# GpSimd splits the weights block by block: order of the halves, constant waits, no gate operation

## The chip, the core and the metric

The kernel runs on one core of one Trainium2 chip. A core has five engines that run at the same time and meet only through semaphores: TensorE (PE in the profile, with PEld for its weight loads) multiplies matrices, VectorE (DVE), ScalarE (ACT) and GpSimd (POOL) work on rows of elements, and SyncE (SP) issues transfers from the chip's main memory. The metric is the device time of one execution in microseconds (us).

## The reference

A decoder of two layers on 512 positions of width 1024, in float32. Each layer has a feed-forward of width 2816, a mixer, a cross-attention into 256 memory positions, and another feed-forward:

```python
for layer in range(DEPTH):
    h = h + 0.5 * swiglu(rmsnorm(h, ffn1_norm[layer]), ...)
    hn = rmsnorm(h, mix_norm[layer])
    if layer % 2 == 0:
        mix = concatenate([gla_mixer(...), s5_mixer(...)]) @ ev_w_out
    else:
        mix = dsa_mixer(hn, ...)            # indexer, top-k, attention
    h = h + mix
    h = h + cross_attn(rmsnorm(h, xa_norm[layer]), mem_n, ...)
    h = h + 0.5 * swiglu(rmsnorm(h, ffn2_norm[layer]), ...)
return rmsnorm(h, final_norm)
```

## The kernel before

**Weights.** All weights come as one stream of 381 blocks of 128 x 1024 float32 (512 KB), in the order of use. A block goes into one of two slots of `raw`, block b into slot b % 2, in two halves of 512 columns, called a and b here. For exactness each weight is split in two: a high part in the fp32r format and a low part, the rest. `W` has two slots as well, each with a high and a low part. A product then is three matmuls (`mm3`, L338 to L340: high by high, high by low, low by high), so an ordinary block is 8 x 3 = 24 matmuls of 512 columns.

**Who does what.** SyncE loads a half of `raw` as soon as GpSimd has split the same half of the block two earlier. GpSimd splits: a TENSOR_SCALAR (L308) writes the high part, a TENSOR_TENSOR (L312) the low part, with a wait on the first between them. Before both stands the gate, a TENSOR_TENSOR on one column (L307), behind the two waits: for the load, and for TensorE to be done with this half of the block two earlier. Four semaphores count halves in order: `half_split` and `split_ready` (a and b halves split), `half_done` and `block_done` (a and b halves used up by TensorE).

**The order of GpSimd.** Two blocks at a time: a of the even, a of the odd, b of the even, b of the odd. Block 108 (`LONE`) stands alone, and the pairs behind it begin with an odd block. Both parts are loops at run time, 53 and 136 turns, whose waits are against registers. SyncE's reloads have the same loops and order.

**The order of TensorE.** Most blocks are used one after the other, a then b (`tile`, `down`, `kv_tile`); TensorE waits for `half_split` at the start and for `split_ready` in the middle. In three places it is otherwise. `project` begins each projection with two blocks interleaved, for k = 0 to 7 both in turn, as the normalised input comes ready in pieces k (`x_lo`), and it waits for the a halves of both first:

```python
pe.wait_ge(S("half_split"), at + 2)
...
for k in range(KC):
    if k == KC // 2:
        pe.wait_ge(split_ready, at + 2)
    pe.wait_ge(S("x_lo"), X_LO_NORM[n] + k + 1)
    for t in range(min(2, nt)):
        m = tile_k(BANKS[t], (at + t) % 2, x, k, k == 0, k == KC - 1)
```

The last two of the 22 down blocks of a feed-forward are interleaved in the same way over the eight output banks, so that the outputs come ready one by one and VectorE can begin the next normalisation (`norm`: L1384 adds to h, L1359 writes the low part of x, L1369 adds squares). The feed-forwards begin at blocks 0, 125, 191 and 315 and have 66 blocks each; behind the first stands the projection of the even mixer (66), behind the second the third feed-forward (191), behind the third the projection of the odd mixer (257). And `glu` (blocks 88 and 89) takes one half block for each of its four outputs.

**The memory keys and values.** `kv_tile` works on 256 columns (the memory), so its matmuls are half as long. Of the first layer, blocks 83 to 87 (keys) come behind the mixer's projections, then `glu`, then three more (90 to 92), then singly between the parts of the gated linear attention (`gla`). ScalarE copies each out of its bank (L1072), and behind the fifth key it computes the decays (L1098), on which VectorE waits (L1682); then come the sigmoids of `glu`.

**The start.** `load(0, a)`, part of x, the vectors, `load(1, a)`, `load(0, b)`, `load(1, b)`, and then the rest of x and the constants.

Of the kernel before, what the change touches and what calls it, by code (L numbers as in the profile page):

```python
# [31 lines left out]
ALU = mybir.AluOpType  # L32
# [3 lines left out]
P = 128  # L36
# [8 lines left out]
HALF = BLK // 2  # L45
# [40 lines left out]
LONE = XQ_AT[0] - 1  # L86
OD_AT, OD_TILES = 257, 16
OD_V_AT = 273
N_BLOCKS = 381
# [88 lines left out]
def build_trunk(nc, xT, memT, pos, vecs, w_alpha, s5b, s5bt, s5c, blocks, mats, mask, rows, stream, out):  # L178
    with ExitStack() as ctx:
        def sb(name, shape, dt=F32):  # L180
            return ctx.enter_context(nc.sbuf_tensor(name, shape, dt))
# [3 lines left out]
        def S(name):  # L185
            if name not in sems:
                sems[name] = ctx.enter_context(nc.semaphore(name))
            return sems[name]
# [5 lines left out]
        raw = sb("w_raw", [P, 2, BLK])  # L194
# [19 lines left out]
        s5_tables = nc.dram_tensor("s5_tables", (4, P, 2 * T), F32, kind="Internal").ap()  # L214
        ident = mat[:, 0, :]
        cmask = mat[:, 3, :]
        gate = sb("gate", [P, 2])
        tiny_i = sb("tiny_i", [P, 16], I32)
        Pt = [ar[:, i * T:(i + 1) * T] for i in range(16)]
        KT = kv[:, 0:4 * T].rearrange("p (n m) -> p n m", m=MEM)  # L220
# [5 lines left out]
        def area(at, n=T):  # L226
            return ar[:, at:at + n]
# [34 lines left out]
        @block.sync  # L262
        def _(sp):
            def load(b, s, half):
                c = slice(half * HALF, (half + 1) * HALF)
                src = stream[b] if isinstance(b, int) else stream[bass.ds(b, 1)].rearrange("a p n -> p (a n)")
                sp.dma_start(raw[:, s, c], src[:, c]).then_inc(S(f"raw{s}{'ab'[half]}"), 16)

            def reload(b, s, half):

                sp.wait_ge(split_ready if half else S("half_split"), b - 1)
                load(b, s, half)

            load(0, 0, 0)
            sp.dma_start(h[:, 0:2, :], xT[:, 0:2, :]).then_inc(S("x_in0"), 16)
            sp.dma_start(vec[:], vecs).then_inc(S("vec_in"), 16)
            load(1, 1, 0)
            load(0, 0, 1)
            load(1, 1, 1)
            sp.dma_start(h[:, 2:8, :], xT[:, 2:8, :]).then_inc(S("x_in1"), 16)  # L280
            sp.dma_start(mat[:], mats).then_inc(S("mat_in"), 16)
            sp.dma_start(msk[:], mask).then_inc(S("msk_in"), 16)
            sp.dma_start(area(A_MEM, 4 * T).rearrange("p (k m) -> p k m", m=MEM), memT).then_inc(S("mem_in0"), 16)
            sp.dma_start(area(A_TIME), rows[0:1, :].to_broadcast([P, T])).then_inc(S("time_in"), 16)
            with sp.Fori(1, LONE // 2) as i:
                for half in range(2):
                    for e in range(2):
                        reload(i * 2 + e, e, half)
            for half in range(2):
                reload(LONE, 0, half)  # L290
            with sp.Fori(LONE // 2, N_BLOCKS // 2) as i:
                for half in range(2):
                    for e in range(2):
                        reload(i * 2 + (e + 1), 1 - e, half)


        @block.gpsimd
        def _(pool):
            def split(b, s, half, count, first=False):

                c = slice(half * HALF, (half + 1) * HALF)
                pool.wait_ge(S(f"raw{s}{'ab'[half]}"), count * 16)
                if not first:

                    pool.wait_ge(S("block_done") if half else S("half_done"), b - 1)

                    pool.tensor_tensor(gate[:, 0:1], gate[:, 1:2], gate[:, 1:2], ALU.add)  # L307
                pool.tensor_scalar(W[:, s, 0, c], raw[:, s, c], 1.0, 0.0, ALU.mult, ALU.add  # L308
                                   ).then_inc(S(f"w_hi{'ab'[half]}"), 1)
                pool.wait_ge(S(f"w_hi{'ab'[half]}"), b + 1)  # L310

                pool.tensor_tensor(W[:, s, 1, c], raw[:, s, c], W[:, s, 0, c].bitcast(F32), ALU.subtract  # L312
                                   ).then_inc(split_ready if half else S("half_split"), 1)

            pool.memset(gate[:], 0.0).then_inc(S("gate_set"), 1)
            pool.wait_ge(S("gate_set"), 1)
            for half in range(2):
                for e in range(2):  # L320
                    split(e, e, half, 1, first=True)
            with pool.Fori(1, LONE // 2) as i:
                for half in range(2):
                    for e in range(2):
                        split(i * 2 + e, e, half, i + 1)
            for half in range(2):
                split(LONE, 0, half, LONE // 2 + 1)
            with pool.Fori(LONE // 2, N_BLOCKS // 2) as i:
                for half in range(2):
                    for e in range(2):  # L330
                        split(i * 2 + (e + 1), 1 - e, half, i + (e + 1))


        @block.tensor
# [1822 lines left out]
```

## Time and profile before

| what | value |
|---|---|
| median of 3 runs | 2364.57 us (2361.61 to 2366.76) |
| the profiled execution | 2365.24 us, its span 2363.4 us |
| TensorE busy | 2251.5 us (95%) |
| GpSimd busy | 1707.6 us (72%), 2287 instructions |
| VectorE busy | 1024.3 us (43%) |
| ScalarE busy | 416.4 us (18%) |
| mean granted TensorE clock | 0.983 |

The span goes from the first to the last instruction; 1.8 us of the execution's time lie around it. Matmuls are pipelined: a matmul of 512 columns is recorded with 0.39 us, but the next starts some 0.23 us after it. The granted clock is a share of 2.4 GHz; 0.50 is 1.2 GHz.

### The profile page before, as it was taken

How to read it: one execution, taken by the hardware profiler on the slowest of the kernel's cores; microseconds unless marked ns; L12 is line 12 of the kernel's file. 1: busy time of each engine (PE TensorE's matmuls, PEld its weight loads, DVE VectorE, ACT ScalarE, POOL GpSimd, SP SyncE). 2: the span in 40 equal slices, each digit the busy share in tenths (PEclk: the TensorE clock that was granted, in tenths of full speed). 3: DMA queues.
4: the chain of work that ended last, by engine and by line, in shares of the span. 5: the costliest groups of instructions: out<-in, count | busy, mean ns of one | idle time of the engine just before them, and what ended most of it. 6: DMA issues, size and time to landing. Idle time of an engine off the chain costs nothing.

```text
span 2363.4 us, 31958 instructions
## 1 busy us (share of the span) xinstructions
PE 2251.5 (95%) x10548; PEld 1827.9 (77%) x10548; DVE 1024.3 (43%) x1327; ACT 416.4 (18%) x721; POOL 1707.6 (72%) x2287
## 2 busy tenths in 40 slices
PE   8999999987999999999999999999987999999997
PEld 6788877877777788887878888877755868888886
DVE  7564675634452432234153223156696434222214
ACT  2111112013121211111131111120223122011111
POOL 7688987648575587887877788777663737878874
PEclk9999999998899999999999999999999999999998
DMA  5233223212222133233322323222221312232332
GB/s 177 88 114 115 91 89 117 86 64 89 72 75 72 58 98 98 93 98 98 111 90 91 98 94 98 93 91 80 75 76 41 96 38 94 98 98 93 98 94 84
DMA packets 114147, 214.08 MB, mean 91 GB/s; under 512 B 12688, under 2 KB 13088, under 8 KB 113696
## 3 DMA queue, kind: packets, MB, share of 16 engines
q1 hardware_dynamic: 110736, 203.61, 27.0%
q10 hardware_dynamic: 3344, 9.52, 1.1%
q8 instruction: 49, 0.80, 0.1%
q14 instruction: 18, 0.15, 0.0%
HBM read 208.89 MB, written 4.19 MB: 90 GB/s over the span
## 4 chain that ended last, share of the span: by engine, by line
PE 77%; DVE 12%; issue 5%; POOL 4%; ACT 1%; DMA 0%; POOLq 0%; SPq 0%; DVEq 0%; ACTq 0%
PE ps L338 24%; PE ps L340 24%; PE ps L339 24%; POOL w_split L312 2%; POOL w_split L308 2%; DVE tg L1369 2%; PE ps L800 1%; DVE arena L1879 1%; DVE col L1878 1%; PE ps L825 1%; DVE x L1359 1%; POOL gate L307 1%; DVE arena L1898 0%; DVE col L1901 0%; DMA h<-in_xT 0%
## 5 line engine op out<-in xcount | busy, mean ns | idle before, releaser
L338 PE MATMUL ps<-x,w_split 128*128 128x512 f32 (+1 forms) x2872 | 1125.5, 392 | 43.8 <-POOL w_split L312 25.3
L339 PE MATMUL ps<-x,w_split 128*128 128x512 f32 (+1 forms) x2872 | 1110.1, 387 | 0.0
L340 PE MATMUL ps<-x,w_split 128*128 128x512 f32 (+1 forms) x2872 | 1110.0, 386 | 0.0
L312 POOL TENSOR_TENSOR w_split<-w_raw,w_split 128x512 fp32r<-128x512 f32 x762 | 1015.8, 1333 | 63.6
L338 PEld LDWEIGHTS ps<-x,w_split 128*128 128x128 f32 x2872 | 545.0, 190 | 171.5 <-POOL w_split L312 31.7
L307 POOL TENSOR_TENSOR gate<-gate 128x1 f32<-128x1 f32 x758 | 243.5, 321 | 563.8 <-PE ps L340 561.0
L339 PEld LDWEIGHTS ps<-x,w_split 128*128 128x128 f32 x2872 | 544.9, 190 | 110.9 <-issue 5.1
L340 PEld LDWEIGHTS ps<-x,w_split 128*128 128x128 f32 x2872 | 544.7, 190 | 108.5
L308 POOL TENSOR_SCALAR w_split<-w_raw 128x512 fp32r<-128x512 f32 x762 | 500.2, 656 | 4.3 <-DMA w_raw<-in_stream 4.3
L1411 DVE TENSOR_TENSOR tu<-ps,rstd 128x512 f32<-128x512 f32 x88 | 60.8, 691 | 350.0 <-PE ps L340 350.0
L1448 DVE TENSOR_TENSOR x<-arena,x 128x512 fp32r<-128x512 f32 x88 | 87.7, 1013 | 246.0 <-ACT x L1028 246.0
L980 ACT ACTIVATE sg<-tg 128x512 f32<-128x512 f32 x88 | 55.6, 632 | 712.9 <-DVE tg L1408 711.2
L1408 DVE TENSOR_TENSOR tg<-ps,rstd 128x512 f32<-128x512 f32 x88 | 60.7, 690 | 212.1 <-PE ps L340 211.2
L1417 DVE TENSOR_TENSOR arena<-sg,tu 128x512 f32 (+1 forms) x88 | 110.4, 1254 | 16.6 <-ACT sg L980 7.6
L1028 ACT ACTIVATE x<-arena 128x512 fp32r (+1 forms) x88 | 53.9, 629 | 332.5 <-PE ps L340 332.5
L1384 DVE SCALAR_TENSOR_TENSOR h<-ps,h 128x512 f32<-128x512 f32 x64 | 44.0, 688 | 149.8 <-PE ps L340 149.4
L942 ACT ACTIVATE x<-h,vec 128x512 fp32r<-128x512 f32 x64 | 46.3, 723 | 208.5 <-DVE h L1384 205.0
L1369 DVE TENSOR_TENSOR tg<-tg,sq 128x512 f32<-128x512 f32 x63 | 70.6, 1121 | 0.1
L1359 DVE SCALAR_TENSOR_TENSOR x<-h,vec,x 128x512 fp32r<-128x512 f32 x64 | 67.7, 1057 | 6.7 <-ACT x L942 6.7
L338 PE MATMUL ps<-w_split,x 128*128 128x256 f32 (+1 forms) x192 | 65.5, 341 | 5.1 <-DVE arena L1486 4.2
L1492 DVE TENSOR_TENSOR arena<-ps,rstd 128x512 f32<-128x512 f32 x32 | 21.9, 691 | 96.5 <-PE ps L340 96.2
L339 PE MATMUL ps<-w_split,x 128*128 128x256 f32 (+1 forms) x192 | 60.5, 315 | 0.0
(259 smaller groups left out, 1374.7 us busy)
## 6 DMA issues: line engine op xcount, KB each, us to landing
w_raw<-in_stream SPq DMA_DIRECT2D x762, 256.0 KB, 2.6
s_tables<-kv ACTq DMA_DIRECT2D x4, 512.0 KB, 3.3
arena<-s_tables ACTq DMA_DIRECT2D x4, 512.0 KB, 5.2
out<-h ACTq DMA_DIRECT2D x8, 256.0 KB, 2.2
h<-in_xT SPq DMA_DIRECT2D x1, 1536.0 KB, 8.5
arena<-in_memT SPq DMA_DIRECT2D x1, 1024.0 KB, 10.1
arena<-in_memT ACTq DMA_DIRECT2D x1, 1024.0 KB, 4.8
h<-in_xT SPq DMA_DIRECT2D x1, 512.0 KB, 4.0
```

What stands on the lines that cost most here:

```text
L307: pool.tensor_tensor(gate[:, 0:1], gate[:, 1:2], gate[:, 1:2], ALU.add)
L308: pool.tensor_scalar(W[:, s, 0, c], raw[:, s, c], 1.0, 0.0, ALU.mult, ALU.add).then_inc(S(f"w_hi{'ab'[half]}"), 1)
L312: pool.tensor_tensor(W[:, s, 1, c], raw[:, s, c], W[:, s, 0, c].bitcast(F32), ALU.subtract).then_inc(split_ready if half else S("half_spli ...
L338: pe.matmul(dst, wh, xh, start=start, stop=False)
L339: pe.matmul(dst, wh, xl, start=False, stop=False)
L340: return pe.matmul(dst, wl, xh, start=False, stop=stop)
L1359: dve.scalar_tensor_tensor(X[to][:, k, 1, :], h[:, k, :], gain(n, k), X[to][:, k, 0, :].bitcast(F32), ALU.mult, ALU.subtract).then_inc(S(" ...
L1369: ins = dve.tensor_tensor(tg[:, 0, :], tg[:, 0, :], sq[:, k % 2, :], ALU.add)
L1408: dve.tensor_tensor(tg[:, s, :], ps[:, BANKS[2 * s], :], rstd[:], ALU.mult).then_inc(S("gate_ready"), 1)
L1411: dve.tensor_tensor(tu[:, s, :], ps[:, BANKS[2 * s + 1], :], rstd[:], ALU.mult).then_inc(S("up_ready"), 1)
L1417: dve.tensor_tensor(dst, sg[:, s:s + 1, :], tu[:, s:s + 1, :], ALU.mult).then_inc(S("hid_done"), 1)
L1448: dve.tensor_tensor(X[xo][:, ch:ch + 1, 1, :], hid[:, d, :], X[xo][:, ch:ch + 1, 0, :].bitcast(F32), ALU.subtract).then_inc(S("x_lo"), 1)
```

## The change

GpSimd's loops are written out: 381 blocks in turn, of each block half a and then half b, with constants in the waits. The gate operation and its tile are gone. SyncE's reloads stay loops, with halves in block order too; its first four loads are as before. Nothing changes on TensorE, VectorE and ScalarE.

```diff
-        gate = sb("gate", [P, 2])
...
             with sp.Fori(1, LONE // 2) as i:
-                for half in range(2):
-                    for e in range(2):
+                for e in range(2):
+                    for half in range(2):
                         reload(i * 2 + e, e, half)
...
             with sp.Fori(LONE // 2, N_BLOCKS // 2) as i:
-                for half in range(2):
-                    for e in range(2):
+                for e in range(2):
+                    for half in range(2):
                         reload(i * 2 + (e + 1), 1 - e, half)
...
-            def split(b, s, half, count, first=False):
-
-                c = slice(half * HALF, (half + 1) * HALF)
-                pool.wait_ge(S(f"raw{s}{'ab'[half]}"), count * 16)
-                if not first:
-
+            def split(b, half):
+
+                s, c = b % 2, slice(half * HALF, (half + 1) * HALF)
+                pool.wait_ge(S(f"raw{s}{'ab'[half]}"), 16 * (b // 2 + 1))
+                if b >= 2:
                     pool.wait_ge(S("block_done") if half else S("half_done"), b - 1)
-
-                    pool.tensor_tensor(gate[:, 0:1], gate[:, 1:2], gate[:, 1:2], ALU.add)
...
-            pool.memset(gate[:], 0.0).then_inc(S("gate_set"), 1)
-            pool.wait_ge(S("gate_set"), 1)
-            for half in range(2):
-                for e in range(2):
-                    split(e, e, half, 1, first=True)
-            with pool.Fori(1, LONE // 2) as i:
+            for b in range(N_BLOCKS):
                 for half in range(2):
-                    for e in range(2):
-                        split(i * 2 + e, e, half, i + 1)
-            for half in range(2):
-                split(LONE, 0, half, LONE // 2 + 1)
-            with pool.Fori(LONE // 2, N_BLOCKS // 2) as i:
-                for half in range(2):
-                    for e in range(2):
-                        split(i * 2 + (e + 1), 1 - e, half, i + (e + 1))
+                    split(b, half)
```

## Rows read from the trace of the kernel before

**Rows 1.** The page, its groups of instructions: the operation that the change deletes.

```profile
L307 POOL TENSOR_TENSOR gate<-gate 128x1 f32<-128x1 f32 x758 | 243.5, 321 | 563.8 <-PE ps L340 561.0
```

**Rows 2.** The waits of the span: us in total, times, longest.

```profile
PE ps L338 <- POOL w_split L312: 26.0, 15, 9.5
```

**Rows 3.** Busy time by engine in a plain stretch of a feed-forward.

```profile
1250.00:1300.00 50.00, 50.00 (x222) 41.42 (x221) 13.04 (x15) 5.73 (x7) 40.37 (x57) 1.00 0.30 94
```

**Rows 4.** Timeline of GpSimd ahead of the memory keys: start, us, operation, idle before.

```profile
517.26 0.19 POOL L307 TENSOR_TENSOR gate<-gate 128x1 f32<-128x1 f32 x1
...
517.42 0.62 POOL L308 TENSOR_SCALAR w_split<-w_raw 128x512 fp32r<-128x512 f32 x1
...
519.37 0.19 POOL L307 TENSOR_TENSOR gate<-gate 128x1 f32<-128x1 f32 x1
...
531.75 0.19 POOL L307 TENSOR_TENSOR gate<-gate 128x1 f32<-128x1 f32 x1 [8.12 <-PE ps L340]
...
534.71 1.27 POOL L312 TENSOR_TENSOR w_split<-w_raw,w_split 128x512 fp32r<-128x512 f32 x1
```

**Rows 5.** Timeline of TensorE and VectorE in the memory keys.

```profile
547.75 0.58 PE L338 MATMUL ps<-x,w_split 128*128 128x256 f32 x1 [3.36 <-POOL w_split L312]
...
554.76 0.28 PE L340 MATMUL ps<-x,w_split 128*128 128x256 f32 x1
...
554.88 0.39 PE L338 MATMUL ps<-x,w_split 128*128 128x512 f32 x1
...
557.45 0.76 DVE L1682 SCALAR_TENSOR_TENSOR arena<-arena,tg 128x512 f32<-128x512 f32 x1 [13.65 <-ACT tg L1098]
...
579.14 0.39 PE L338 MATMUL ps<-x,w_split 128*128 128x256 f32 x1 [1.58 <-POOL w_split L312]
```

**Rows 6.** Timeline at the end of the first feed-forward, three engines.

```profile
377.79 0.40 PE L338 MATMUL ps<-x,w_split 128*128 128x512 f32 x1
...
401.33 0.50 PE L338 MATMUL ps<-x,w_split 128*128 128x512 f32 x1 [0.71 <-DVE x L1359]
...
388.81 0.62 POOL L308 TENSOR_SCALAR w_split<-w_raw 128x512 fp32r<-128x512 f32 x1
...
391.77 0.62 POOL L308 TENSOR_SCALAR w_split<-w_raw 128x512 fp32r<-128x512 f32 x1
...
387.01 1.78 DVE L1369 TENSOR_TENSOR tg<-tg,sq 128x512 f32<-128x512 f32 x1
```

**Rows 7.** TensorE behind an idle stretch; granted clock is the third column from the end.

```profile
496.26 0.80 PE L338 MATMUL ps<-w_split,x 128*128 128x512 f32 x1 [4.22 <-DVE arena L1486]
...
498.00:499.00 1.00, 1.00 (x4) 0.71 (x4) 1.00 (x3) 0.00 (x0) 0.00 (x0) 0.50 0.00 0
...
500.00:501.00 1.00, 1.00 (x6) 0.80 (x5) 1.00 (x2) 0.50 (x1) 0.14 (x1) 1.00 0.00 0
```

**Rows 8.** Timeline of the start, GpSimd and TensorE.

```profile
7.14 0.62 POOL L308 TENSOR_SCALAR w_split<-w_raw 128x512 fp32r<-128x512 f32 x1 [1.62 <-DMA w_raw<-in_stream]
...
9.39 0.79 POOL L308 TENSOR_SCALAR w_split<-w_raw 128x512 fp32r<-128x512 f32 x1
...
9.47 0.79 PE L338 MATMUL ps<-x,w_split 128*128 128x512 f32 x1 [9.47 <-POOL w_split L312]
...
22.48 0.50 PE L338 MATMUL ps<-x,w_split 128*128 128x512 f32 x1 [0.68 <-DVE x L1359]
```

**Rows 9.** TensorE's waits from 268 to 336 us; a stretch of the second layer's keys.

```profile
PE ps L338 <- POOL w_split L312: 3.9, 4, 1.2
...
PE ps L338 <- DVE x L1448: 2.6, 2, 1.6
...
1710.00:1720.00 10.00, 8.71 (x61) 7.33 (x60) 9.55 (x20) 2.14 (x5) 9.58 (x15) 1.00 0.34 110
```

**Rows 10.** The chain that ended last, from 1606.9 to 1609 us, at a loop's turn.

```profile
1608.05 0.07 POOL w_split L312
...
1608.39 0.04 POOLq L305
```

## Prediction

> **What bounds the kernel now.** I read four views. First the page, for the groups of instructions: the gate operation that the change deletes is a 128x1 add, run 758 times, 243.5 us of GpSimd's busy time [rows 1]. That is the obvious saving, so the next question is whether GpSimd holds anyone up. The waits answer it: TensorE stood idle for GpSimd's second operation (L312) for 26.0 us in 15 waits, the longest 9.5 us [rows 2]. Of these 9.47 us are the start [rows 8], so 16.5 us are spread over 14 waits. In a plain stretch (1250 to 1300 us) TensorE has no idle time: 222 matmuls in 50 us, 0.225 us each, while GpSimd is busy 40.4 of 50 us [rows 3]. A block of 24 matmuls is then 5.4 us, half a block 2.7 us. So over most of the span faster splitting is worth nothing. What counts is where a split lands last, before and after.
>
> **The order.** A half can be split only when TensorE has used the same half of the block two earlier. Before, GpSimd goes a(2i), a(2i+1), b(2i), b(2i+1). b(2i) stands behind a(2i+1), whose buffer comes free only half way through block 2i-1; b(2i) is done just before it is used. In the new order it is done half a block to a block earlier. The reverse holds where TensorE needs both a-halves at once: now a(n+1) stands behind b(n).
>
> **Part 1, the gate.** Halves in a row are 2.11 us apart from gate to gate, and the gate's start lies 0.16 us before that of the next operation [rows 4]; without it 1.96 us. Where VectorE works with two SBUF operands at the same time, the two engines wait for each other: halves are 2.96 us apart and a VectorE add takes 1.78 us [rows 6]. There the gate stands in the time in which VectorE has its turn, and the first real operation would stand in it instead; I count nothing. Elsewhere the 0.15 us lies under TensorE's blocks, except in part 2.
>
> **Part 2, the memory keys (blocks 83 to 92), a gain.** Their matmuls have 256 columns and follow each other by 0.12 us [rows 5], so a block takes 24 x 0.12 = 2.9 us, less than two splits: GpSimd is the bound. Until 531.75, when half of block 83 was done, GpSimd stood idle for 8.12 us, although b(84) could have been split in that time; its second operation ran only at 534.71 [rows 4]. In the new order b(84) is ready at the start. From 531.75 on the six halves 85a to 87b take 6 x 1.96 = 11.8 us, to 543.6, and the last half block 1.5 us: the five key blocks end at 545.1 instead of 554.88 [rows 5], 9.8 us earlier. Part of that is the clock: TensorE stood idle 3.36 us until 547.75, and the matmul behind it is recorded with 0.58 us, where those at full clock have 0.28 [rows 5]. The next ten halves (gated unit's blocks 88 and 89, keys 90 to 92) take 19.6 us more, plus about 2.1 us for VectorE's turns, to 565.3; with the last half block 566.8, where the old order ended at 579.14 + 1.44 = 580.6 [rows 5]. Gain 13.8 us. Is something else late next? ScalarE and VectorE compute the decays in this stage, and VectorE started only at 557.45, after 13.65 us of waiting for ScalarE [rows 5], which waits for the copy of the fifth key block and so moves with it. Their results, ready 7 us after that start, and the four sigmoids behind them (some 4 us) would be there by 559 to 561. So they don't take the gain back. I take 13.3; bounds 8 (VectorE's turns in all halves) and 16.
>
> **Part 3, the other waits.** One of 0.63 us in the mixer goes. In 268 to 336 us TensorE waits 3.9 us for GpSimd but also 2.6 us for VectorE's low halves, at the end [rows 9]: VectorE works there without a break and sets when the stage ends. 0.5 us. In the second layer's keys VectorE is busy 9.55 of 10 us [rows 9] and sets the pace: 0. Together 1.1 us, bounds 0 and 5.
>
> **Part 4, the end of a feed-forward, a loss three times.** The last two down blocks (64 and 65) run interleaved, from 377.79 [rows 6], 48 matmuls of 0.227 us, to 388.7. The projection behind them interleaves 66 and 67, so it starts only when a(66) and a(67) are both split. Before, both were split in the second half of the pair, and TensorE went on without a gap. In the new order a(67) stands behind b(66), which needs all of block 64: its last matmul is number 45 of 48, at 388.0. Then b(66) and a(67) take 2 x 2.96 = 5.9 us, as VectorE normalises at this time: TensorE starts at 393.9, 5.2 us idle. The pair's own 10.9 us then end at 404.8. Before, the pair waited for the normalisation (the last part at 401.33 [rows 6], end 402.8): so 2.0 us are lost, the rest was slack. But such an idle stretch costs the clock: after 4.22 us idle until 496.26 the granted clock was 0.50 (1.2 of 2.4 GHz) in 498 to 499 and 1.00 in 500 to 501 [rows 7], some 3.3 us at half rate, 1.6 us of work. Together 3.6 us. The same pattern stands at blocks 191 and 257: 3 x 3.6 = 10.8 us. Bounds: 2.0 each if the clock stays (6), 5.4 each if it is low twice as long (16). The fourth feed-forward has nothing behind it.
>
> **Part 5, the start, a loss.** TensorE's first block also wants a(0) and a(1). The first loads are not reordered. a(1) was split from 7.14, when its load landed, to 9.4 [rows 8]; now b(0) comes first. Its load stands behind a(1)'s on the queue: at the earliest 7.14, at the latest 9.39 (GpSimd took it then without a wait), some 7.8 by the rate of the loads. Then 2 x 2.35 us: TensorE starts at 12.5 in place of 9.47, 3.0 us late. 0.68 us of it were waited for VectorE later on [rows 8], so 2.3; bounds 0.2 (the clock, low in the first 5 us, rises at the same instant) and 3.9.
>
> **Part 6, loops and loads.** 189 turns of GpSimd's loop vanish. The register and branch work runs from 1608.05 to 1608.39, under the operation of 1.3 us and more that began at 1608.05 [rows 10]: 0. The Trainium skill (Advanced Engine Details and Errata, Control Flow Timing) puts a compare-and-branch at about 108 ns; 189 of them would be an estimated 20 us if they stood in the way, and by the row they don't. SyncE's loads follow the splits' order, each still two blocks ahead: 0.
>
> **The sum:** -13.3 - 1.1 + 10.8 + 2.3 = -1.3 us, on the profiled execution's 2365.24 us as on the median of 2364.57 (0.7 us below it): 2363.3 us. 0.2% is 4.7 us, about what a measurement can tell.
>
> **Rivals.**
> - A, the new waits win (slower). TensorE's clock stays low for two stretches after each stall at a feed-forward's end: 16 us; or the keys give back only 8. The point is where three stalls plus the start pass the keys' gain by 4.7 us, 6.3 us each. 16 + 2.3 - 13.3 - 1.1 = +3.9; with the keys at 8, +9: 2374. For it: the stalls are longer than the ones seen to lower the clock. Against: the pair had slack for 3 us.
> - B, the keys win (faster). The stalls cost 2 us each (the clock or VectorE's spare time takes the rest; GpSimd's idle 2.8 us before 388.0 lets VectorE run ahead by 1.1), VectorE's stage gives 2 of its 3.9 back: -13.3 - 2.6 + 6 + 1.5 = -8.4: 2356.
> - C, the change does nothing: GpSimd's waits only move, the keys being held by ScalarE's copies and decays, and the pair by VectorE: 2364.6, within my forecast's class. Against: the gaps at the keys are put down to L312.
> - D, the written-out code stalls GpSimd: 762 halves of some four instructions must be fetched once. The Trainium skill (Runtime: NRT & Kernel Launch, Instruction fetch mechanics) says that straight code streams in and that crossing a block is mostly hidden. A stall of up to the 2.7 us of half a block would be hidden by the time that each half now has to spare; only in the keys it would count. Ten longer ones of 2.5 us on the path are +25: 2390.
>
> **How the numbers follow.** The forecast's cancellation (with C) 0.48; B 0.27; A 0.22; D 0.03. The range takes in A and B and the bounds of the large terms: 2351 to 2375.
>
> **What would show it.** The gate row gone and GpSimd busy some 240 us less (less in locked stretches). TensorE's idle at the keys nearly gone, and the first matmul of the gated unit, at 554.88 before, some 10 us earlier against the start of the keys. Three waits for L312 of about 5 us at the first matmul after a feed-forward, with a low clock behind. A first matmul at 12.5. If these waits are absent, the order argument is wrong; if they are there and the total still moves, the sizes of clock and keys are.

## The result and the profile after

The changed kernel takes 2376.86 us, the median of 5 runs (2372.26 to 2378.49), against 2364.57 for the kernel before, timed beside it on the same chip: ratio 1.005, 95% interval 1.0037 to 1.0064. It is 12.3 us slower, where 2363.3 was predicted: outside the range of 2351 to 2375, and on the side of rival A.

The page of the profiled execution (2376.86 us, span 2375.1, mean clock 0.979), its busy times, GpSimd's groups and the costliest of VectorE's:

```profile
PE 2253.1 (95%) x10548; PEld 1831.4 (77%) x10548; DVE 1093.3 (46%) x1327; ACT 415.8 (18%) x721; POOL 1539.5 (65%) x1528
...
L308 POOL TENSOR_TENSOR w_split<-w_raw,w_split 128x512 fp32r<-128x512 f32 x762 | 1039.5, 1364 | 63.7
L304 POOL TENSOR_SCALAR w_split<-w_raw 128x512 fp32r<-128x512 f32 x762 | 502.9, 660 | 746.9 <-PE ps L322 740.5
...
L1430 DVE TENSOR_TENSOR x<-arena,x 128x512 fp32r<-128x512 f32 x88 | 120.7, 1388 | 216.6 <-ACT x L1010 216.6
```

GpSimd lost the gate's 243.5 us [rows 1] but only 168.1 us of its busy time. The two real operations take 26.4 us more, and the other 49 us were overlap: before, records of neighbouring operations overlapped, and the page counts such time once. (High part: L308 before, L304 now. Low part: L312 before, L308 now.) VectorE is busy 69 us longer for the same 1327 instructions. TensorE's waits, the groups that matter:

```profile
PE ps L320 <- POOL w_split L308: 32.8, 12, 12.9
...
PE ps L320 <- DVE x L1430: 9.1, 5, 2.7
```

The wait for GpSimd grew from 26.0 [rows 2] to 32.8 us, in fewer and longer waits: 12.9 at the start, three of 4.9, the rest in the memory keys. TensorE's timeline has them:

```profile
12.85 0.80 PE L320 MATMUL ps<-x,w_split 128*128 128x512 f32 x1 [12.85 <-POOL w_split L308]
...
397.69 0.79 PE L320 MATMUL ps<-x,w_split 128*128 128x512 f32 x1 [4.90 <-POOL w_split L308]
...
549.28 0.39 PE L320 MATMUL ps<-x,w_split 128*128 128x256 f32 x1 [1.47 <-POOL w_split L308]
...
555.88 0.50 PE L320 MATMUL ps<-x,w_split 128*128 128x512 f32 x1 [0.27 <-POOL w_split L308]
...
573.35 0.39 PE L320 MATMUL ps<-x,w_split 128*128 128x256 f32 x1 [1.00 <-POOL w_split L308]
```

The first matmul stands at 12.85 in place of 9.47 [rows 8]. At 397.69 is the stall that was forecast behind the first feed-forward. In the keys the waits of 3.36 and 1.58 us [rows 5] have shrunk to 1.47 and 1.00, and the first matmul of the gated unit stands at 555.88, 1.0 us after that of before, although TensorE entered the stage 8.1 us late.

**A ledger by stage.** Both kernels issue the same 10,548 matmuls, so the start of the n-th one can be compared between traces (in e9 without its added ones). The sum goes to the last matmul but one; the profiled executions as a whole differ by 11.6 us. The table gives how much each stage grew against the profiled execution of before, in us; the stages are named by the times of before. The columns behind "changed" are kernels of the next section.

| stage | forecast | changed | changed again | e2 | e1 | e7 | e3 | e9 |
|---|---|---|---|---|---|---|---|---|
| start, to 64.58 | +2.3 | +4.7 | +4.3 | +6.0 | +0.9 | +1.7 | +5.6 | +4.9 |
| 64.58 to 377.79 | -0.5 | -0.7 | -0.8 | +0.2 | -1.7 | -0.1 | -0.7 | -0.7 |
| three feed-forward ends | +10.8 | +12.9 | +13.1 | +16.8 | -0.3 | +0.2 | -3.2 | +5.9 |
| memory keys, 525.82 to 582.89 | -13.3 | -9.9 | -9.8 | -7.0 | -5.3 | -0.2 | -8.7 | -8.9 |
| linear attention, to 657.69 | 0 | +5.5 | -0.4 | -0.6 | -2.1 | +4.6 | -0.2 | +3.9 |
| all the rest | -0.6 | -0.5 | +1.2 | +6.0 | +4.2 | +0.1 | +0.8 | +0.3 |
| sum | -1.3 | +12.0 | +7.6 | +21.4 | -4.3 | +6.3 | -6.4 | +5.4 |

The linear attention is not the change's doing: e7, which has the old order and the gate, is 4.6 us longer there too, and e8, the changed kernel again, isn't. Its mean clock differs from one execution to the next: 0.83 before, 0.79 after, and 0.86 in another execution of the same changed kernel. The windows of this stage (the mean clock is the third column from the end) of before, of the changed kernel and of the changed kernel again:

```profile
583.00:658.00 75.00, 65.17 (x358) 53.86 (x359) 34.58 (x49) 12.09 (x19) 33.46 (x49) 0.83 0.19 63
```

```profile
581.00:661.30 80.30, 69.23 (x358) 56.92 (x358) 38.01 (x48) 11.70 (x18) 35.47 (x37) 0.79 0.22 65
```

```profile
580.30:654.70 74.40, 63.43 (x358) 53.00 (x358) 35.83 (x48) 11.79 (x18) 35.66 (x37) 0.86 0.22 69
```

So a single trace says what a wait costs, but its total is good to some 5 us only; totals are taken from medians.

### The profile page after: what moved, and what is told of

The parts are those of the page before. It is cut to its first block, busy times and chain, and to the rows that moved or that the text cites. A ratio compares the mean times of both kernels' runs of the same rounds, so it can differ in the third digit from the quotient of the medians.

```text
span 2375.1 us, 30115 instructions
## 1 busy us (share of the span) xinstructions
PE 2253.1 (95%) x10548; PEld 1831.4 (77%) x10548; DVE 1093.3 (46%) x1327; ACT 415.8 (18%) x721; POOL 1539.5 (65%) x1528
## 4 chain that ended last, share of the span: by engine, by line
PE 85%; DVE 9%; POOL 2%; ACT 1%; issue 1%; DMA 0%; SPq 0%; DVEq 0%; ACTq 0%; POOLq 0%
PE ps L320 26%; PE ps L322 26%; PE ps L321 26%; POOL w_split L308 1%; PE ps L782 1%; DVE arena L1861 1%; DVE col L1860 1%; PE ps L807 1%; POOL w_split L304 1%; PE ps L697 1%; DVE arena L1880 0%; DVE x L1430 0%; DVE col L1883 0%; PE ps L463 0%; DVE arena L1891 0%
## 5 line engine op out<-in xcount | busy, mean ns | idle before, releaser
L320 PE MATMUL ps<-x,w_split 128*128 128x512 f32 (+1 forms) x2872 | 1122.9, 391 | 50.4 <-POOL w_split L308 32.8
L308 POOL TENSOR_TENSOR w_split<-w_raw,w_split 128x512 fp32r<-128x512 f32 x762 | 1039.5, 1364 | 63.7
L304 POOL TENSOR_SCALAR w_split<-w_raw 128x512 fp32r<-128x512 f32 x762 | 502.9, 660 | 746.9 <-PE ps L322 740.5
L1430 DVE TENSOR_TENSOR x<-arena,x 128x512 fp32r<-128x512 f32 x88 | 120.7, 1388 | 216.6 <-ACT x L1010 216.6
L1399 DVE TENSOR_TENSOR arena<-sg,tu 128x512 f32 (+1 forms) x88 | 125.5, 1426 | 20.5 <-ACT sg L962 11.6
L1351 DVE TENSOR_TENSOR tg<-tg,sq 128x512 f32<-128x512 f32 x63 | 79.6, 1263 | 0.1
L320 PE MATMUL ps<-w_split,x 128*128 128x256 f32 (+1 forms) x192 | 66.9, 348 | 4.2 <-DVE arena L1468 4.2
L1374 DVE RECIPROCAL rstd<-std 128x512 f32<-128x512 f32 x9 | 30.2, 3353 | 71.7 <-ACT std L952 71.7
L321 PE MATMUL ps<-w_split,x 128*128 128x256 f32 (+1 forms) x192 | 62.1, 323 | 0.0
L322 PE MATMUL ps<-w_split,x 128*128 128x256 f32 (+1 forms) x192 | 61.6, 321 | 0.0
## 6 DMA issues: line engine op xcount, KB each, us to landing
arena<-in_memT SPq DMA_DIRECT2D x1, 1024.0 KB, 10.3
```

What stands on the lines that cost most here:

```text
L320: pe.matmul(dst, wh, xh, start=start, stop=False)
L321: pe.matmul(dst, wh, xl, start=False, stop=False)
L322: return pe.matmul(dst, wl, xh, start=False, stop=stop)
L1351: ins = dve.tensor_tensor(tg[:, 0, :], tg[:, 0, :], sq[:, k % 2, :], ALU.add)
L1399: dve.tensor_tensor(dst, sg[:, s:s + 1, :], tu[:, s:s + 1, :], ALU.mult).then_inc(S("hid_done"), 1)
L1430: dve.tensor_tensor(X[xo][:, ch:ch + 1, 1, :], hid[:, d, :], X[xo][:, ch:ch + 1, 0, :].bitcast(F32), ALU.subtract).then_inc(S("x_lo"), 1)
```

## The experiments

Eight kernels ran, each in 5 rounds beside the kernel before: e1, e7, e3 and e5 on one chip (before: 2366.94 us, 24 runs), the other four on another (before: 2365.56 us, 17 runs). "Pairs" means the old order a, a, b, b over two blocks.

| kernel | order of the halves | gate | median us (range, runs) | ratio to before, 95% |
|---|---|---|---|---|
| e7 | pairs | yes | 2367.23 (2360.7 to 2370.64, 12) | 1.0002 (0.9989 to 1.0014) |
| e1 | pairs | no | 2360.03 (2352.69 to 2367.81, 12) | 0.9971 (0.9956 to 0.9985) |
| e2 | by block | yes | 2385.36 (2382.11 to 2387.23, 6) | 1.0077 (1.0062 to 1.0092) |
| e8, the changed kernel again | by block | no | 2375.83 (2372.45 to 2378.8, 6) | 1.004 (1.0024 to 1.0056) |
| e3 | by block, pairs at the three ends | no | 2356.55 (2355.12 to 2357.98, 6) | 0.9955 (0.9939 to 0.9971) |
| e5 | as e3, and a pair at the start | no | 2355.9 (2352.57 to 2361.05, 7) | 0.9954 (0.9938 to 0.997) |
| e6 | pairs, by block in blocks 82 to 95 | no | 2358.25 (2355.09 to 2359.27, 6) | 0.9962 (0.9947 to 0.9976) |
| e9 | by block, extra matmuls in the stall | no | 2366.49 (2362.62 to 2370.91, 12) | 1.0 (0.999 to 1.0009) |

**e1: the old order alone put back.** The written-out code, its constant waits and the missing gate stay; splits and reloads go in pairs again (the reloads' loops are left out here).

```diff
-            for b in range(N_BLOCKS):
-                for half in range(2):
-                    split(b, half)
+            def pair(*blocks):
+                for half in range(2):
+                    for b in blocks:
+                        split(b, half)
+            for b in range(0, LONE, 2):
+                pair(b, b + 1)
+            pair(LONE)
+            for b in range(LONE + 1, N_BLOCKS, 2):
+                pair(b, b + 1)
```

> Written-out splits with constant waits and no gate, but in the order of the kernel before (a, a, b, b of two blocks, loads too). If the order is the cause of the loss (first theory), this is back at the kernel before or a little below it: 2360 to 2365 us, no wait of 4.9 us at the ends of the feed-forwards, a first matmul at 9.5 us, and the keys' waits for GpSimd are back (some 10 us). If writing out the code or deleting the gate is the cause (rival), it stays near 2377 us.

2360.03 us: 16 us below the changed kernel, 7 below before. The expectation's first branch holds. The loss is all in the order of the halves (splits and reloads together), and the rest of the change is a gain. The table shows no loss at the ends (-0.3) and the start (+0.9), and of the gain in the keys 5.3 us are there without the new order.

**e7: e1 with the gate put back.** The gate's tile comes back too. What is left of the change then is that the loops are written out, with constants in the waits.

```diff
                 if b >= 2:
                     pool.wait_ge(S("block_done") if half else S("half_done"), b - 1)
+                    pool.tensor_tensor(gate[:, 0:1], gate[:, 1:2], gate[:, 1:2], ALU.add)
```

> As the run before, in the old order, with the gate operation put back in front of each split: the kernel before but for the loops and the registers in the waits. If loops cost nothing, 2362 to 2367 us, the same as the kernel before. The difference from the run without the gate is the gate's own price: 0 by the prediction; where VectorE and GpSimd take turns the changed kernel showed halves 2.69 us apart and not 2.96, which would make the gate cost 2 to 4 us over the whole.

Ratio 1.0002, and the interval allows some 3 us either way. So the loops with their register waits, against fetching the written-out code, make no difference that can be measured, and the 7.2 us between e7 and e1 are the gate: more than the 2 to 4 that I had expected at most. In the ledger the difference is 5.1 us in the keys and 1.6 between 64.58 and 377.79. (The gate taken out with the loops kept was not tried.)

**e2: the changed kernel with the gate.** The same edit, in the new order.

> The changed kernel with the gate operation put back in front of each split. In the old order the gate was worth 7 us (2367.2 with it, 2360.0 without). If it costs where GpSimd is the bound (the keys, 16 halves of 0.15 us) and where the two engines take turns (0.27 us a half at the three ends of a feed-forward and in 268 to 336 us), it costs 4 to 7 us here too: 2381 to 2384 us. If the new order has made GpSimd's pace harmless (rival), 2377.

2385.36 against e8's 2375.83 on the same chip: here the gate costs 9.5 us, more than the 4 to 7 expected. By the ledger 2.8 are in the keys and 1.7 at the start (another 4.8 in "all the rest" of this one execution), and 3.7 at the ends, where the halves of a stall now lie 3.51 us apart and TensorE waits 6.6 us. GpSimd's timeline, and the matmul that waited:

```profile
394.47 0.60 POOL L305 TENSOR_TENSOR gate<-gate 128x1 f32<-128x1 f32 x1 [2.47 <-PE ps L326]
...
397.98 0.64 POOL L305 TENSOR_TENSOR gate<-gate 128x1 f32<-128x1 f32 x1
...
401.61 0.80 PE L324 MATMUL ps<-x,w_split 128*128 128x512 f32 x1 [6.60 <-POOL w_split L310]
```

**e8: the changed kernel again**, unaltered, on the chip of e2, e6 and e9.

> The changed kernel on the chip of these runs, to set the others against. The mended ends gave 20 us by the medians, where the stalls and the clock behind them add up to 12.9 us by the traces. If the difference is this trace's own luck with the clock in the linear attention (34 us at half rate from 583 to 658 us), another trace shows less there and the median comes out near 2370; if the new order brings it about, 2377 and 34 us again.

2375.83 us, ratio 1.004 (first measurement 1.005). Its ledger agrees with the changed kernel's to 0.5 us in the start, the ends and the keys, and differs by 5.8 us in the linear attention. Neither branch of the expectation holds whole: this execution did have less of the low clock there, but it is the fastest of the six, and the median stayed near the second branch's. The order of splits and reloads together therefore costs 16 to 18 us, with the gate (e7 to e2) or without it (e1 to e8), and the missing gate gives 7 to 9.5 back.

**e3: pairs only at the three ends.** Blocks 66 and 67, 191 and 192, 257 and 258 are split a, a, b, b; all others by block. The loads stay by block.

```diff
+            b = 0
+            while b < N_BLOCKS:
+                if b in (66, 191, 257):
+                    pair(b, b + 1)
+                    b += 2
+                else:
+                    pair(b)
+                    b += 1
```

> The changed kernel, but at blocks 66, 191 and 257 with the next block in the order a, a, b, b. First theory: the three idle stretches of 4.9 us and the half clock behind them go, 4.2 us each by the milestones, so 12.5 us less than the changed kernel: some 2364 us. If the slow clock and the stall only cover a wait for VectorE (rival), less than 5 us.

2356.55 us, ratio 0.9955 where the changed kernel has 1.005 and 1.004: three pairs of 381 blocks are worth some 20 us, more than the 12.5 I had expected. TensorE has no wait for GpSimd at the ends and its clock stays at 1.00, where in the changed kernel it fell. The windows of e3 and of the changed kernel around the first end:

```profile
386.00:412.00 26.00, 24.54 (x108) 19.18 (x107) 22.29 (x24) 11.83 (x19) 19.06 (x16) 1.00 0.24 78
```

```profile
393.00:398.00 5.00, 0.31 (x1) 0.31 (x2) 5.00 (x6) 2.52 (x5) 4.83 (x5) 0.77 0.16 52
398.00:400.00 2.00, 2.00 (x6) 1.52 (x6) 2.00 (x4) 0.56 (x2) 1.92 (x2) 0.50 0.40 129
400.00:402.00 2.00, 2.00 (x6) 1.61 (x5) 2.00 (x3) 1.98 (x3) 0.34 (x1) 0.50 0.19 46
402.00:404.00 2.00, 2.00 (x9) 1.56 (x9) 0.76 (x2) 0.38 (x1) 0.00 (x0) 0.87 0.24 87
404.00:406.00 2.00, 2.00 (x11) 1.65 (x10) 0.00 (x0) 0.00 (x0) 0.76 (x2) 1.00 0.03 8
```

In the changed kernel the half rate (0.50, 1.2 GHz) covers the time from some 395.7 to some 402.5 us: it began in the stall and lasted through the first 4.8 us of the work behind it. Against before, e3 even gains 1.1 us at each end. GpSimd stands idle there for 2.77 us until 387.72, and of VectorE's additions of squares (L1361, in before L1369) only five take turns with it, at 1.78 us, where before and e1 have six; the sixth takes 0.68. That is the size of the 1.1 us that rival B named. The expectation compared a stall with none; between the changed kernel and e3 it is 4.3 + 1.1 us an end, 16 in all. The other 4 of the 20 us by the medians are not placed.

**e9: the clock kept up through the stall.** The changed kernel, with 20 matmuls of 128 columns (ones by ones, into a bank that the projection's first product overwrites) ahead of the wait at the three ends. The split is as late as ever.

```diff
+                if n in (1, 4, 5):
+                    for s, v in waits0:
+                        pe.wait_ge(s, v)
+                    for _ in range(20):
+                        pe.matmul(ps[:, BANKS[0], 0:P], ones[:], ones[:], start=True, stop=True)
                 pe.wait_ge(S("half_split"), at + 2)
```

> The changed kernel with 20 matmuls of 128 columns more (ones by ones, into a bank that is free and is written anew afterwards) ahead of the wait at the three ends of a feed-forward, so that TensorE works through the stall. The stall of 4.9 us stays; if the half clock behind it costs 2.4 us each (first theory), 6 to 7 us less than the changed kernel. If the stall alone is the loss, no change, or slower by what the added matmuls reach beyond the stall.

2366.49 us, 9.3 below e8 on the same chip, where 6 to 7 were expected; the ledger has 7.2 of them at the ends. The timeline at the first end shows the extra matmuls as one row (each of the 20 is recorded as two), and the projection behind them at the same place as in the changed kernel (397.93, there 397.69):

```profile
392.86 4.63 PE L358 MATMUL ps<-ones 128*128 128x128 f32 x40
...
397.93 0.50 PE L320 MATMUL ps<-x,w_split 128*128 128x512 f32 x1 [0.45 <-POOL w_split L308]
```

And e9's windows there:

```profile
393.00:398.00 5.00, 4.55 (x42) 4.36 (x40) 5.00 (x7) 2.51 (x5) 4.83 (x5) 1.00 0.20 53
398.00:400.00 2.00, 2.00 (x9) 1.65 (x10) 2.00 (x4) 0.63 (x2) 1.92 (x2) 1.00 0.37 125
```

The clock is 1.00 and each end costs 1.94 to 1.98 us in place of 3.92 to 4.61 (e8). That splits the price of an end: 2.0 us for the stall itself, 2.4 for the clock.

**e5: a pair at the start as well.** The edit against e3:

```diff
-                if b in (66, 191, 257):
+                if b in (0, 66, 191, 257):
```

> As the run before, and blocks 0 and 1 too in the order a, a, b, b. First theory: another 2 to 4 us less, 2360 to 2362 us, with the first matmul at 9.5 us. If the keys' gain of 9.9 us is kept whole, it is faster than the kernel before by up to 9 us (2356); if the linear attention behind the keys gives 5 us back, as in the changed kernel, by 3 to 4 us.

2355.9 against 2356.55, on the same chip: no difference beyond the spread, where another 2 to 4 us less were expected. In the traces the start gives 1.4 us. The first matmul is back at 10.02 (e3: 12.78), but at the matmul at 60.19 of before e5 is still 2.4 us late, e3 3.9. So the start's loss has a second part, which the order of blocks 0 and 1 doesn't touch.

**e6: the new order only around the keys.** Splits in the old order elsewhere; loads by block. The edit against e3:

```diff
-                if b in (66, 191, 257):
+                if not 82 <= b < 96 and b != LONE:
```

> No gate, the old order of pairs everywhere but for blocks 82 to 95, which go block by block (the memory keys of the first layer and the gated unit). If the new order's gain sits in the keys alone, it keeps what the kernel with three mended ends has: 2354 to 2357 us, against 2360 us with pairs everywhere. If the gain of block order lies in the stage from 268 to 336 us as well, it stays at 2358 or above.

2358.25 us: ratio 0.9962, e1's was 0.9971, and the intervals overlap. The expectation's rule (2358 or above) would put a gain of the new order between 268 and 336 us as well, but the ledger doesn't bear it out: from 64.58 to 377.79 the old order gains 1.7 us without the gate (e1 and e6), the new one 0.7. The trace has the gain in its place (-10.3 in the keys, e1 -5.3). Against e1 it is 1.9 us later at the start, 1.1 in the linear attention and 0.8 in "all the rest", where both lose 4 to 5 us and e3 only 0.8; why is open. That the order is worth 4 to 5 us in the keys rests on the traces' matmuls there, not on the totals.

## Why the prediction was wrong

The steps were there with their signs; the forecast was that they cancel to -1.3 us. Two losses were put too small and the one large gain too large, and all three errors point the same way: by the ledger the four terms of the sum come to +7.0 us. The keys miss by 3.4 us, the start by 2.4, the ends by 2.1.

**Part 4 (ends), mechanism right, size 12.9 for 10.8.** The idle time (4.90 for 5.2) and its net loss (2.0, e9) came as worked out. The term that failed is the clock: I took 3.3 us of work at half rate from a shorter idle stretch [rows 7], and it was 4.8 at the first end and 5.2 at the other two (the granted clock was 0.50 until 1204.6 and 1576.7, the work began at 1199.4 and 1571.5), so 2.4 to 2.6 us in place of 1.6. That is rival A's mechanism, at less than the full price that it was given. (The rival's turning point of 6.3 us a stall leaves the start out; with it, (13.3 + 1.1 - 2.3 + 4.7) / 3 is 5.6.) Halves behind each other were 2.69 us apart, not 2.96:

```profile
392.28 1.01 POOL L304 TENSOR_SCALAR w_split<-w_raw 128x512 fp32r<-128x512 f32 x1 [3.14 <-PE ps L322]
...
394.92 1.06 POOL L304 TENSOR_SCALAR w_split<-w_raw 128x512 fp32r<-128x512 f32 x1
```

**Part 2 (keys), gain 9.9 for 13.3.** From GpSimd's first half after the wait (538.90) to the first matmul of the gated unit it took 17.0 us, where I had 13.3. I let the first six halves run at 1.96 us, as if VectorE stood still. It doesn't: during the third and the fourth key block it computes the linear attention's scans, and three of the halves then take 3.21, 3.15 and 2.69 us. GpSimd's and VectorE's timelines of the changed kernel:

```profile
540.86 0.62 POOL L304 TENSOR_SCALAR w_split<-w_raw 128x512 fp32r<-128x512 f32 x1
...
542.83 1.08 POOL L304 TENSOR_SCALAR w_split<-w_raw 128x512 fp32r<-128x512 f32 x1
544.00 2.07 POOL L308 TENSOR_TENSOR w_split<-w_raw,w_split 128x512 fp32r<-128x512 f32 x1
546.04 1.06 POOL L304 TENSOR_SCALAR w_split<-w_raw 128x512 fp32r<-128x512 f32 x1
...
549.19 1.06 POOL L304 TENSOR_SCALAR w_split<-w_raw 128x512 fp32r<-128x512 f32 x1
```

```profile
543.47 1.51 DVE L1655 TENSOR_TENSOR_SCAN arena<-arena,tu 128x512 f32<-128x512 f32 x1
...
546.65 1.52 DVE L1655 TENSOR_TENSOR_SCAN arena<-arena,tu 128x512 f32<-128x512 f32 x1
```

The same scans stood in the trace of before, at 536.57 and 539.91; I had read VectorE there only by the end of its 13.65 us of waiting [rows 5]. The Trainium skill (SBUF — State Buffer, "SBUF: two separate sides") calls the port pair of the two engines an exclusive lock that is held for a whole instruction; these rows agree: GpSimd's low part takes 2.07 us beside VectorE's operations on two operands, and 1.29 us where VectorE is idle. And part of the 9.9 is not the order's: the gate alone was 5.1 us here (e7 to e1), where Part 1 and Part 2 gave it 0.15 us a half, 2.4 for 16 halves. From the first half behind the wait to the twentieth GpSimd takes 49.7 us in e7 and 45.2 in e1, 0.24 us a half with the waits in between; where VectorE is busy the gate itself is recorded with 0.64 us. At the gated unit's first matmul the gain was 7.1 us, where I had 9.8, and behind it 2.9 for 4.0.

**Part 5 (start), loss 4.7 for 2.3.** The first matmul is 3.4 us late for 3.0, and at the end of the first pair of blocks 1.7 are left, less than said. What I didn't look for came later: another 1.8 us until the matmul at 63.72 (before 60.19), and 1.2 behind it, where the clock was low. The chain there goes through VectorE's operations on 16 columns, which stand ahead of ScalarE's squares. Their group, in the changed kernel and in e1 (the same operation, other line numbers):

```profile
L1513 DVE TENSOR_TENSOR tiny<-tiny 128x16 f32<-128x16 f32 x12 | 6.2, 517 | 0.4
```

```profile
L1520 DVE TENSOR_TENSOR tiny<-tiny 128x16 f32<-128x16 f32 x12 | 2.1, 175 | 0.4
```

517 ns each for 175: some of these operations of 0.17 us wait for GpSimd's turn to end. This group grew most; all 46 operations on these tiles together take 18.3 us, where e1 has 16.7 and before 16.3, which is the size of the 1.8 us. The matmul that they delay, after an idle time of 4.30 us (before 2.48), runs at a mean clock of 0.68:

```profile
63.72 5.92 PE L463 MATMUL ps<-sq,ones 128*128 128x256 f32 x16 [4.30 <-ACT sq L1036]
```

```profile
63.70:69.00 5.30, 5.28 (x15) 3.21 (x15) 0.46 (x1) 2.87 (x8) 0.00 (x0) 0.68 0.02 6
```

The 1.8 us go with the order of the splits: e5 has them without the late first matmul, and e1 and e6, which split in pairs there, haven't (e6 loads by block, so the loads' order isn't it). That the even spacing of the splits is the cause is only what these groups suggest, and no run moved the spacing alone. The 1.2 us of the clock are not bound to the order. e7 and e6 lose 1.1 and 1.3 us at the same place in the old order, at a clock of 0.50, and e6's idle time is that of e1, whose clock stayed at 1.00. The same matmuls in e6 and in e1:

```profile
61.73 6.04 PE L473 MATMUL ps<-sq,ones 128*128 128x256 f32 x16 [2.21 <-ACT sq L1046]
```

```profile
61.13 4.75 PE L470 MATMUL ps<-sq,ones 128*128 128x256 f32 x16 [2.21 <-ACT sq L1043]
```

All six traces with the new order at this place lose to the clock here, but these two lose to it without that order, so how much of the 1.2 us is the order's stays open.

**Part 3, the number right:** -0.7 between 64.58 and 377.79, for -0.5. From 268 us on TensorE's waits for GpSimd (3.9 us) went, and those for VectorE's wide additions, which became slower (1388 ns for 1013), grew from 2.6 to 6.3. The order itself gave nothing there: e1, with the old order and no gate, gains 1.7. **Part 6, right:** e7 shows that the written-out loops are worth nothing within 3 us, and with it falls rival D's 25 us. The order of the loads was not changed alone; e6, with new loads and old splits outside the keys, shows no gain from it. **Part 1** was right at an end in the old order: e1, without the gate, has halves 2.96 us apart too. It was wrong in the new order (3.51 us with the gate, 2.69 without) and in the keys.

**The range** ended at 2375, and 2376.86 was measured. Each of the four terms lies inside its own bounds except the start's (4.7, bound 3.9); their sum of +7.0 would have been inside the range as well. What carried the median over it is the rest: 12.3 us for the changed kernel and 10.3 for e8, against 7.0 from the terms. The traces put that rest into the linear attention's clock (5.5 us in one execution, -0.4 in the other) and into small shifts, which single executions can't attribute. This stays open.

## What to carry to other kernels

Before an order is changed for the sake of one stage, list every place where the consumer needs two things at once, and price the idle time there with the clock behind it: three stalls of 4.9 us cost 12.9 us and hid a change that is otherwise 10 us faster than before (e3, e5: 0.45%; some 7 of them are the missing gate). Where two engines take turns, count a half by the timeline of the other engine in that very stretch, not by its mean rate. And separate the parts of an edit: here loops gave nothing, leaving out the gate gave 7 us, and the order took 16.

## What the runs showed of the hardware

- **An instruction of one column is not free next to a busy VectorE.** The gate takes 0.19 us alone and 0.6 us in turns. In the old order VectorE is busy 1028.9 us with it (e7) and 1013.4 without (e1). But in the new order VectorE is faster with it: with it (e2) VectorE is busy 982.5 us, without it (e8) 1091.9, and the addition of 512 columns in the feed-forwards takes 834 ns in place of 1390. The groups of e2 and of e8:

```profile
L1434 DVE TENSOR_TENSOR x<-arena,x 128x512 fp32r<-128x512 f32 x88 | 72.0, 834 | 264.2 <-ACT x L1014 264.2
```

```profile
L1430 DVE TENSOR_TENSOR x<-arena,x 128x512 fp32r<-128x512 f32 x88 | 120.9, 1390 | 218.2 <-ACT x L1010 218.2
```

 TensorE doesn't wait for most of these, so the 109 us gained nothing: e2 is the slowest kernel of all.
- **Idle time costs more than itself.** 4.90 us idle were followed by 4.8 to 5.2 us of work at 1.2 GHz; 20 useless matmuls in each of the three gaps kept the clock at 2.4 GHz and made the kernel 9.3 us faster. After 2.21 us idle the clock fell in one kernel (e6) and stayed in another (e1).
- **The linear attention's clock is luck.** In it TensorE works with gaps, and the mean clock of the stage was 0.79 and 0.86 in two executions of one kernel, 5.8 us apart.
